# Grid attention with q and k projected by feature: no turns, a new order on VectorE, and parts cut one step apart

## The chip, the cores and the metric

The kernel runs on one core of one Trainium2 chip. The metric is the device time of one execution in microseconds (us), as the median of the runs shown. The core has TensorE (PE in the profile; PEld is its weight load), VectorE (DVE), ScalarE (ACT), GpSimd (POOL) and SyncE (SP); each runs its own queue of instructions in order, and they wait for each other by semaphores. Data lies in SBUF (128 partitions); TensorE writes its results to PSUM, eight banks of 512 float32 values per partition.

## The reference

Two blocks of two layers each, on 512 tokens of width 1024 (the second block has 256 context tokens besides), all in float32. The part that the change touches is the last layer of the second block: 16 heads of 64 attend from a grid of 8 rows x 64 columns to a window of neighbours, with a relative bias, and to all context tokens.

```python
def neighbourhood_latent(q, k, v, kc, vc, rpb):
    ...
        s_loc = jnp.einsum('bqhd,bkhd->bhqk', qr, kr).astype(jnp.float32) * scale + bias.astype(jnp.float32)
        s_loc = jnp.where(mask, s_loc, -jnp.inf)
        s_ctx = jnp.einsum('bqhd,blhd->bhql', qr, kc).astype(jnp.float32) * scale
        p = jax.nn.softmax(jnp.concatenate([s_loc, s_ctx], axis=-1), axis=-1)
        p_loc = p[..., :kh * GRID_W].astype(vr.dtype)
        p_ctx = p[..., kh * GRID_W:].astype(vc.dtype)
        return jnp.einsum('bhqk,bkhd->bqhd', p_loc, vr) + jnp.einsum('bhql,blhd->bqhd', p_ctx, vc)

def c_mixer(u, uc, in_w, out_w, rpb, need_ctx):
    ...
    o = neighbourhood_latent(q, k, v, k_c, v_c, rpb)
    y = (o * jax.nn.silu(z)) @ out_w
```

With 8 grid rows and a window 8 rows high, each query sees all 512 latent keys, masked by column, and 256 context keys: 768 in all.

## The kernel before

The kernel is a list of stages (`layers`, `block_two`), played one after the other on every engine. A stage waits for the one before it, unless it is `joined`.

**Precision.** Float32 products are made of three fast ones. Each operand is split into a high part (rounded to the format `fp32r`, by a ScalarE copy) and a low part (operand minus high part, on VectorE). `three` (line 516) issues high x high, high x low and low x high into the same bank.

**Products** (`Product`). Weights come in pieces of 1 MB through two buffers `w_raw`; ScalarE cuts `w_high` (L476), VectorE `w_low` (L481), and TensorE multiplies while the next piece is cut. In mode "tok" the tokens are stationary, 128 at a time, and the result has tokens on partitions. In mode "feat" the weights are stationary and the result has features on partitions; with 768 tokens (`spill`) each feature tile needs two banks, one of 512 and one of 256 columns. The stages ahead of the grid attention make the gate z (feat), q, k and v (all tok), each in two groups. `CopyOut` copies finished banks out, by turns on ScalarE and VectorE (L1125, L1127, L1129).

**Grid attention** (`WidePairs` with `grid=True`, built by `grid_units`). It has 8 units, a unit being two heads (`m` = 0, 1), and 4 query blocks of 128 in each, so 32 steps. A step's scores for both heads fill three banks (512 latent keys, 256 context keys, 256 context keys, 512 latent keys); steps use banks 0 to 2 and 3 to 5 by turns. Bank 6 collects the output of a unit, bank 7 is for small turns. In iteration s:

- TensorE: `scores(s + 1)` (12 matmuls, L1822, which wait until the banks of step s - 1 have been copied out by both engines), `turn_probs(s)` (12 transposes of 128x128 back into the same banks, L1856; the first four wait for the first head's exp, the others for the second's), one `turn` of q or k of the next unit (L1801), `values(s - 1)` (24 matmuls, L1873), and at the end of a unit `wide` (L1881): four transposes of the inverse sums, which wait for `staged_ready`.
- VectorE: at the end of a unit `gate_wide` (L2095, inverse sums times gate z) and `invert` (L2052 reciprocal, L2057 widening copy, which signals `staged_ready`); `maxima(s + 1)`: the maximum over the context columns (L2023, `sink_part`), then per head one pass that adds the bias in place and takes the maximum (L2034) and a negation (L2036); `copy_probs(s)` (L2064, the first bank of turned probabilities, signals `turned_ready`); `low_turned` (L2073, L2079), the low part of what was turned.
- ScalarE: `copy_probs(s)` (L1945, the other two banks), `copy_turned` (L1921, the high part of what was turned), `exps(s + 1)` (L1934, two, one per head), and at the end of a unit the copy of the output (L1952) and the issue of the loads of z (L1967) and of bias tiles (L1972).
- GpSimd: the final product of a unit (L2131) and the mask on a bias tile (L2141).

q and k lie by token in `q_c` and `k_c`, but the scores need them by feature, with q's columns in each grid row reversed. So for every unit TensorE turns 128 columns of q (4 transposes) and of k (4 and 2) through bank 7 ("turns"; the entries of `turns` name the iteration), ScalarE copies the high part to `q_high` and `k_high`, and VectorE writes the low part in place over the turned columns:

```python
turns.append((4 * p - 4, p, q_high[:, p % 2, 0:4, :], lambda x, p=p: q_c[:, x, P * p:P * p + P], P, 4, None, "back"))
```

The three turns of the first unit stand ahead of the loop, followed by ten matmuls without use (`keep_warm`, L523).

## Time and profile before

| | |
|---|---|
| median of 3 runs (lowest, highest) | 2335.25 us (2334.78, 2335.45) |
| the profiled execution | 2336.09 us |
| its span | 2334.3 us |
| busy: TensorE, VectorE, ScalarE, GpSimd | 2248.6 (96%), 1297.0 (56%), 925.0 (40%), 272.2 (12%) us |
| chain that ended last | PE 80%, DVE 10%, ACT 5% |
| mean granted clock of TensorE | 0.994 |

The span is the stretch from the first to the last instruction of one profiled execution; that execution took 1.8 us more than its span, and 0.84 us more than the median. All times of rows count from the start of the span. Matmuls are pipelined, so a matmul's duration overlaps with that of the next; the distance of two starts tells what one costs. TensorE's 96% is therefore no proof that it is the bound everywhere: the chain of work that ended last is followed back from the last instruction, at each step to whatever released it, and it shows who was waited for. Products fill most of the span; the grid attention runs from about 2112 to 2282 us. A row of a timeline gives start, duration, engine, line, operation, what it writes and reads, its shape and, in brackets, the idle time before it with what ended it. "ACTq" and "issue" are the time of an engine's instruction queue, not of its arithmetic.

### The profile page before, as it was taken

How to read it: one execution, taken by the hardware profiler on the slowest of the kernel's cores; microseconds unless marked ns; L12 is line 12 of the kernel's file. 1: busy time of each engine (PE TensorE's matmuls, PEld its weight loads, DVE VectorE, ACT ScalarE, POOL GpSimd, SP SyncE). 2: the span in 40 equal slices, each digit the busy share in tenths (PEclk: the TensorE clock that was granted, in tenths of full speed). 3: DMA queues.
4: the chain of work that ended last, by engine and by line, in shares of the span. 5: the costliest groups of instructions: out<-in, count | busy, mean ns of one | idle time of the engine just before them, and what ended most of it. 6: DMA issues, size and time to landing. Idle time of an engine off the chain costs nothing.

```text
span 2334.3 us, 32859 instructions
## 1 busy us (share of the span) xinstructions
PE 2248.6 (96%) x13409; PEld 1859.1 (80%) x13409; DVE 1297.0 (56%) x1890; ACT 925.0 (40%) x1564; POOL 272.2 (12%) x175
## 2 busy tenths in 40 slices
PE   6999999999999999999999999999899999999998
PEld 5876688888888776788888888897787878887777
DVE  4687458963225778369943255216666363126774
ACT  3447742222214357542222232324655242115663
POOL 2001222211002012132211000000000000001220
PEclk9999999999999999999999999999999999999999
DMA  5210035532223210145523321320000224213321
GB/s 157 86 68 2 1 104 182 184 109 90 108 94 94 81 37 2 37 144 171 172 90 108 108 65 51 101 87 13 15 15 15 93 82 141 72 55 75 54 57 55
DMA packets 146088, 191.10 MB, mean 82 GB/s; under 512 B 42229, under 2 KB 95490, under 8 KB 145922
## 3 DMA queue, kind: packets, MB, share of 16 engines
q1 hardware_dynamic: 110288, 169.83, 22.0%
q10 hardware_dynamic: 35586, 19.01, 3.5%
q8 instruction: 106, 1.74, 0.3%
q14 instruction: 44, 0.36, 0.0%
q0 software_dynamic: 64, 0.16, 0.0%
HBM read 181.51 MB, written 7.48 MB: 81 GB/s over the span
## 4 chain that ended last, share of the span: by engine, by line
PE 80%; DVE 10%; ACT 5%; issue 3%; DMA 1%; POOL 1%; ACTq 1%; POOLq 0%; DVEq 0%
PE ps L516 63%; PE ps L1822 3%; PE ps L2391 2%; PE ps L2408 2%; DVE ps L2034 2%; PE ps L2420 2%; DVE probs_t L2064 1%; DVE neg_max L2015 1%; ACT probs L1934 1%; PE ps L1856 1%; PE ps L2396 1%; PE ps L723 1%; DVE sink_part L2023 1%; DVE w_low L481 1%; ACT probs_t L2497 1%
## 5 line engine op out<-in xcount | busy, mean ns | idle before, releaser
L481 DVE TENSOR_TENSOR w_low<-w_raw,w_high 128x2048 fp32r<-128x2048 f32 (+4 forms) x140 | 305.7, 2184 | 497.9 <-ACT w_high L476 497.7
L476 ACT ACTIVATE w_high<-w_raw 128x2048 fp32r<-128x2048 f32 (+4 forms) x140 | 252.9, 1807 | 614.0 <-PE ps L516 603.5
L516 PE MATMUL ps<-h_hi,w_high 128*128 128x512 f32 x976 | 371.7, 381 | 1.6 <-DVE h_lo L2788 0.8
L516 PE MATMUL ps<-h_lo,w_high 128*128 128x512 f32 x976 | 369.1, 378 | 0.0
L516 PE MATMUL ps<-h_hi,w_low 128*128 128x512 f32 x976 | 369.0, 378 | 0.0
L516 PE MATMUL ps<-w_high,h_hi 128*128 128x512 f32 (+3 forms) x736 | 277.4, 377 | 7.8 <-DVE w_low L481 7.1
L516 PE MATMUL ps<-w_low,h_hi 128*128 128x512 f32 (+3 forms) x736 | 274.7, 373 | 0.0
L516 PE MATMUL ps<-w_high,h_lo 128*128 128x512 f32 (+3 forms) x736 | 274.6, 373 | 0.0
L516 PEld LDWEIGHTS ps<-h_hi,w_high 128*128 128x128 f32 x976 | 183.7, 188 | 37.6 <-DVE w_low L481 1.9
L516 PEld LDWEIGHTS ps<-h_hi,w_low 128*128 128x128 f32 x976 | 183.6, 188 | 34.8
L516 PEld LDWEIGHTS ps<-h_lo,w_high 128*128 128x128 f32 x976 | 183.7, 188 | 34.1 <-issue 0.5
L516 PEld LDWEIGHTS ps<-w_high,h_hi 128*128 128x128 f32 x736 | 138.9, 189 | 36.5 <-DVE w_low L481 7.8
L516 PEld LDWEIGHTS ps<-w_low,h_hi 128*128 128x128 f32 x736 | 138.8, 189 | 22.6
L516 PEld LDWEIGHTS ps<-w_high,h_lo 128*128 128x128 f32 x736 | 138.9, 189 | 21.6
L710 DVE SCALAR_TENSOR_TENSOR ada_acc<-ada_w,cond,ada_acc 128x512 f32<-128x512 f32 x168 | 143.6, 896 | 2.5
L1462 POOL TENSOR_TENSOR gated<-gated,inv_wide 128x512 f32<-128x512 f32 x44 | 95.3, 2186 | 374.2 <-ACT gated L1454 374.2
L516 PE MATMUL ps<-act_hi,w_low 128*128 128x512 f32 x352 | 137.0, 389 | 0.0
L516 PE MATMUL ps<-act_hi,w_high 128*128 128x512 f32 x352 | 136.9, 389 | 0.0
L516 PE MATMUL ps<-act_lo,w_high 128*128 128x512 f32 x352 | 136.9, 389 | 0.0
L1934 ACT ACTIVATE probs<-ps,neg_max 128x768 f32<-128x768 f32 (+3 forms) x160 | 123.6, 783 | 13.7 <-DVE neg_max L2019 7.9
L1945 ACT ACTIVATE probs_t<-ps 128x1024 f32<-128x1024 f32 (+2 forms) x68 | 56.0, 823 | 131.7 <-PE ps L1856 131.7
L1457 ACT ACTIVATE act_hi<-gated 128x512 fp32r<-128x512 f32 x44 | 27.7, 632 | 198.3 <-DVE gated L1475 197.3
(360 smaller groups left out, 3905.3 us busy)
## 6 DMA issues: line engine op xcount, KB each, us to landing
w_raw<-in_w_gate_up SPq DMA_DIRECT2D x44, 1024.0 KB, 5.1
ada_w<-in_ada_w SPq DMA_DIRECT2D x24, 1024.0 KB, 5.1
w_raw<-in_w_down SPq DMA_DIRECT2D x20, 1024.0 KB, 4.8
w_raw<-in_w_in SPq DMA_DIRECT2D x16, 1024.0 KB, 5.1
w_raw<-in_c_in_w SPq DMA_DIRECT2D x16, 1024.0 KB, 5.6
w_raw<-in_w_out SPq DMA_DIRECT2D x8, 1024.0 KB, 4.8
w_raw<-in_ab_in_w SPq DMA_DIRECT2D x8, 1024.0 KB, 5.1
bias<-bias_scratch ACTq DMA_DIRECT2D x32, 224.0 KB, 4.8
```

What stands on the lines that cost most here:

```text
L476: e.activation(w_high[j % 2][:, 0:size], w_raw[j % 2][:, 0:size], ACT.Copy).then_inc(sig.w_high_done, 1)
L481: e.tensor_tensor(w_low[j % 2][:, 0:size], w_raw[j % 2][:, 0:size], w_high[j % 2][:, 0:size].bitcast(F32), ALU.subtract).then_inc(sig.w_lo ...
L516: mm = e.matmul(dst, lhs, rhs, start=start and a == 0, stop=stop and a == 2)
L710: ins = e.scalar_tensor_tensor(out=acc, in0=w, scalar=c, in1=acc, op0=ALU.mult, op1=ALU.add)
L1462: e.tensor_tensor(gated[:, m, :], gated[:, m, :], inv_wide[:], ALU.mult).then_inc(sig.silu_scaled, 1)
L1822: return e.matmul(dst.rearrange("p (b c) -> p b c", c=P), q(m, block), k(m, a, b), start=n == 0, stop=stop and n == 2)
L1934: ins = e.activation(self.probs[s % 2][:, r * n:(r + 1) * n], self.row(s, r), ACT.Exp, bias=neg_max2[:, c:c + 1], accum_out=sums2[:, c:c + 1])
L1945: e.activation(self.probs_t[s % 2][:, a:b], flat[:, self.base(s) + a:self.base(s) + b], ACT.Copy).then_inc(sig.turned_second, 1)
L2034: ch.step(e.tensor_tensor_reduce(a, a, bias, 1.0, seed2[:, c], ALU.add, ALU.max, max2[:, c]))
L2391: e.matmul(ps[:, self.bank(s, m), 0:n], q[x.rows(m), t * P:n], k[x.rows(m), 0:n], start=True, stop=False)
L2408: mm = e.transpose(ps[:, self.bank(s, m), kt * P:(kt + 1) * P], probs1[s % 3][:, m, kt * P:(kt + 1) * P], ident)
L2420: mm = e.matmul(ps[64 * m:64 * m + 64, 6, t * P:(t + 1) * P], x.value(m, kt), probs_t1[s % 2][:, m, kt * P:(kt + 1) * P], start=kt == 0, s ...
```

## The change

**q and k by feature.** Both products change to mode "feat": q is scaled and reversed by column when it is copied out, and k is made with two banks per feature tile. The turns, their copies and low parts go, and with them the ten `keep_warm` matmuls ahead of the loop.

**Parts.** The high part of a unit's q and k is now one ScalarE copy each from `q_c` and `k_c` (SBUF), the low part one VectorE subtraction each in place (512 and 768 columns). For the first unit this is done in a new stage `PairAhead` between the products of k and v, into buffers of its own. For unit p the high parts of q and k stand behind the exps in iterations 4p - 5 and 4p - 4 (`cut_at`), the low parts at the end of VectorE's iterations 4p - 4 and 4p - 3.

**Order on VectorE.** In iteration s: context maximum of step s + 1, copy of the turned probabilities of step s, the two bias passes of step s + 1, then `invert`, `gate_wide` and the low part.

```diff
-        q_c = at("q_c", [P, NT, DM], F32, B1)
-        k_c = at("k_c", [P, NA, DM], F32, B1 + 16384)
+        q_c = at("q_c", [P, KD, S], F32, B1)
+        k_c = at("k_c", [P, KD, ALL], F32, B1 + 16384)
...
+        q_first = at("q_first", [P, NT, P], F32R, B1 + 65536)
+        k_first = at("k_first", [P, NA, P], F32R, ROWS_AT)
...
+                self.cut_at = {4 * p - 5 + c: (p, c) for p in range(1, U) for c in range(2)} if grid else {}
...
-                keep_warm(e, 6, 10 if self.grid else 4)
+                if not self.grid:
+                    keep_warm(e, 6, 4)
...
+                    if s in self.cut_at:
+                        p, c = self.cut_at[s]
+                        if p >= 2:
+                            e.wait_ge(sig.scores_ready, B["scores_ready"] + 4 * (p - 2) + 4)
+                        pair_high(e, p, c)
...
+                def context_max(s):
+                    two, b = slice(self.col[s], self.col[s + 1]), self.base(s)
+                    e.wait_ge(sig.scores_ready, B["scores_ready"] + s + 1)
                     ch.step(e.tensor_reduce(out=seed2[:, two], in_=flat[:, b + 512:b + 1024].rearrange("p (m n) -> p m n", m=2),
                                             op=ALU.max, axis=AX.X))
+
+                def grid_max(s, m):
+                    (u, js), b = self.steps[s], self.base(s)
                     j = js[0]
-                    if j == 0:
+                    if j == 0 and m == 0:
                         e.wait_ge(sig.bias_masked, B["bias_masked"] + u)
                     ch.wait(e)
...
+                def grid_iteration(s):
+                    if s == self.N:
+                        gate_piece(e, {n: B[n] for n in ("gate_landed", "pair")}, 1, gate_row, 3)
+                    if s + 1 < self.N:
+                        context_max(s + 1)
+                    if 0 <= s < self.N:
+                        copy_probs(s)
+                    if s + 1 < self.N:
+                        grid_max(s + 1, 0)
+                        grid_max(s + 1, 1)
+                    if s in self.ends:
+                        invert(self.ends[s])
+                    if s - 1 in self.ends:
+                        gate_wide(self.ends[s - 1])
+                    if s - 1 in self.cut_at:
+                        p, c = self.cut_at[s - 1]
+                        pair_low(e, B, p, c, 2 * (p - 1) + c + 1)
...
+        def pair_high(e, p, c):
+            src, high, _ = pair_parts(p, c)
+            e.activation(high, src, ACT.Copy).then_inc(sig.qk_high, 1)
+
+        def pair_low(e, B, p, c, n):
+            src, high, low = pair_parts(p, c)
+            e.wait_ge(sig.qk_high, B["qk_high"] + n)
+            e.tensor_tensor(low, src, high.bitcast(F32), ALU.subtract).then_inc(sig.qk_ready, 1)
...
-            from_in("tok", 0, 512, CopyOut(lambda i, m, t0: q_c[:, m, ds(i * 512, 512)], HD ** -0.5), w="c_in_w_2", groups=2, joined=True),
-            from_in("tok", DM, 512, CopyOut(lambda i, m, t0: k_c[:, m, ds(i * 512, 512)]), w="c_in_w_2", groups=2, tokens=ALL, joined=True),
+            from_in("feat", 0, 512, CopyOut(lambda i, m, t0: q_c[:, i * 4 + m, :].rearrange("p (r c) -> p r c", c=64), HD ** -0.5, view=backwards),
+                    w="c_in_w_2", groups=2, joined=True),
+            from_in("feat", DM, 512, CopyOut(lambda i, m, t0: k_c[:, i * 4 + m, t0:(S if t0 == 0 else ALL)]), w="c_in_w_2", groups=2, tokens=ALL, joined=True),
+            PairAhead(),
```

VectorE at the end of the first unit, in the kernel before (`sums_194` and `inv_stage_192` belong to that unit; the reduction, the two `ISA` passes with their read-outs and negations are the maxima of the next unit's first step; `probs_t` is the copy of turned probabilities):

```order
L2052 RECIPROCAL sums_inv_195<-sums_194 128x8 [waits probs_ready]
L2057 COPY inv_stage_192<-sums_inv_195 128x512 [waits vec_steps]
L2023 TENSOR_REDUCE sink_part<-ps 128x2 [waits scores_ready]
L2034 ISA ps,max_197<-ps,bias_1_154,sink_part 128x512 [waits bias_masked,vec_steps]
L2034 ISA max_197 128x1
L2036 TENSOR_SCALAR neg_max_193<-max_197 128x1 [waits vec_steps]
L2034 ISA ps,max_197<-ps,bias_1_154,sink_part 128x512
L2034 ISA max_197 128x1
L2036 TENSOR_SCALAR neg_max_193<-max_197 128x1 [waits vec_steps]
L2064 COPY probs_t_1_169<-ps 128x512 [waits o_ready,probs_turned]
```

and now:

```order
L2032 TENSOR_REDUCE sink_part<-ps 128x2 [waits scores_ready]
L2075 COPY probs_t_1_169<-ps 128x512 [waits o_ready,probs_turned]
L2045 ISA ps,max_199<-ps,bias_1_154,sink_part 128x512 [waits bias_masked,vec_steps]
L2045 ISA max_199 128x1
L2047 TENSOR_SCALAR neg_max_195<-max_199 128x1 [waits vec_steps]
L2045 ISA ps,max_199<-ps,bias_1_154,sink_part 128x512 [waits vec_steps]
L2045 ISA max_199 128x1
L2047 TENSOR_SCALAR neg_max_195<-max_199 128x1 [waits vec_steps]
L2063 RECIPROCAL sums_inv_197<-sums_196 128x8 [waits probs_ready]
L2068 COPY inv_stage_194<-sums_inv_197 128x512 [waits vec_steps]
```

The copy of turned probabilities moved from behind the two bias passes to ahead of them, and the reciprocal and its widening copy from ahead of the maxima to behind them.

TensorE at the start of the grid stage, before (`con` is the identity matrix, `band_r,ident_r` the matmuls without use, the last row the first scores):

```order
L1801 MATMUL ps<-con,q_c 128x128 [waits evac_vec,bank_done,evac_act]
L1801 MATMUL ps<-con,q_c 128x128 x3
L1801 MATMUL ps<-con,k_c 128x128 x6
L523 MATMUL ps<-band_r,ident_r 128x384 x10
L1822 MATMUL ps<-k_high,q_high 128x512 [waits qk_ready]
```

and now:

```order
L1826 MATMUL ps<-k_first,q_first 128x512 [waits evac_vec,bank_done,evac_act,qk_ready]
L1826 MATMUL ps<-k_first,q_first 128x256
L1826 MATMUL ps<-kc_low,q_first 128x256
L1826 MATMUL ps<-kc_low,q_first 128x512
L1826 MATMUL ps<-k_first,qc_low 128x256
```

The ten transposes and the ten matmuls without use are gone, and the stage's first matmul is one of the scores.

## Rows read from the trace of the kernel before

**Rows 1.** The chain that ended last, grid attention: start us, us, what
```profile
2133.21 1.42 PE ps L1822 x9
...
2158.64 1.43 PE ps L1822 x9
2160.09 0.70 DVE sink_part L2023
...
2163.67 1.43 PE ps L1822 x9
...
2270.77 1.41 PE ps L1822 x9
```
**Rows 2.** Timeline, end of the third unit, TensorE's weight loads and VectorE
```profile
2174.05 0.19 PEld L1822 LDWEIGHTS ps<-k_high,q_high 64*128 64x128 f32 x2 [1.05 <-DVE kc_low L2079]
...
2174.70 0.20 DVE L2052 RECIPROCAL sums_inv<-sums 128x8 f32<-128x8 f32 x1 [0.70 <-ACT probs L1934]
...
2175.01 0.43 DVE L2057 COPY inv_stage<-sums_inv 128x512 f32<-128x512 f32 x1
...
2175.39 1.30 PEld L1856 LDWEIGHTS ps<-con,probs 128*128 128x128 f32 x12
...
2176.37 0.76 DVE L2034 CUSTOM_DVE_ANT_0 ps<-ps,bias,sink_part 128x512 f32<-128x512 f32 x1 [0.17 <-DVE sink_part L2023]
2176.86 1.29 PEld L1873 LDWEIGHTS ps<-probs_t,v_c 128*64 128x64 f32 x24 [0.17 <-issue]
...
2177.38 0.76 DVE L2034 CUSTOM_DVE_ANT_0 ps<-ps,bias,sink_part 128x512 f32<-128x512 f32 x1
...
2178.32 0.42 PEld L1881 LDWEIGHTS ps<-con,inv_stage 128*128 128x128 f32 x4 [0.17 <-issue]
2178.32 0.69 DVE L2064 COPY probs_t<-ps 128x512 f32<-128x512 f32 x1
```
**Rows 3.** Timeline, first steps of the stage
```profile
2112.05 0.42 PEld L1801 LDWEIGHTS ps<-con,q_c 128*128 128x128 f32 x4 [1.41 <-issue]
...
2113.47 0.33 ACTq L1967 DMA_DIRECT2D z_unit<-z_scratch  x1
...
2113.82 3.35 ACTq L1972 DMA_DIRECT2D bias<-bias_scratch  x4
...
2117.38 0.76 DVE L2034 CUSTOM_DVE_ANT_0 ps<-ps,bias,sink_part 128x512 f32<-128x512 f32 x1 [0.17 <-DVE sink_part L2023]
...
2118.49 0.90 ACT L1934 ACTIVATE probs<-ps,neg_max 128x768 f32<-128x768 f32 x1
...
2123.88 0.91 ACT L1934 ACTIVATE probs<-ps,neg_max 128x768 f32<-128x768 f32 x1
...
2124.93 0.86 PEld L1856 LDWEIGHTS ps<-con,probs 128*128 128x128 f32 x8 [0.32 <-ACT probs L1934]
...
2126.06 1.02 ACT L1945 ACTIVATE probs_t<-ps 128x1024 f32<-128x1024 f32 x1 [1.18 <-PE ps L1856]
```
**Rows 4.** Stretches: us, busy by engine (instructions), granted clock, DMA share, GB/s
```profile
1880.00:1890.00 10.00, 8.78 (x46) 7.74 (x44) 4.82 (x13) 1.99 (x5) 0.00 (x0) 0.83 0.00 0
2128.00:2271.00 143.00, 132.31 (x1437) 111.92 (x1438) 110.28 (x265) 90.11 (x169) 32.84 (x13) 1.00 0.32 60
```
**Rows 5.** The chain again: a 768-token feature product, then the products before the grid
```profile
1486.57 67.15 PE ps L516 x384
...
1949.91 161.17 PE ps L516 x711
```
**Rows 6.** Timeline at 701 us: VectorE with and without GpSimd beside it
```profile
700.90 0.74 DVE L1587 SCALAR_TENSOR_TENSOR h_lo<-x_t,cols,h_hi 128x512 fp32r<-128x512 f32 x1
...
703.87 1.18 DVE L1587 SCALAR_TENSOR_TENSOR h_lo<-x_t,cols,h_hi 128x512 fp32r<-128x512 f32 x1
...
701.33 8.30 POOL L1598 TENSOR_TENSOR square_sum<-square_sum,gated 128x512 f32<-128x512 f32 x5 [122.29 <-ACT gated L1572]
```
**Rows 7.** Timeline behind the grid: low parts from SBUF, back to back
```profile
2284.50 4.91 DVE L1657 TENSOR_TENSOR oc_lo<-o_all,oc_hi 128x512 fp32r<-128x512 f32 x8 [3.87 <-ACT oc_hi L1650]
```

More of the change, by code:

```diff
@@ L180, in build_program @@
         con = fixed("con", [P, CONST_W])
+        ROWS_AT = off[0]
         rows = fixed("rows", [P, DEPTH, ROW_W])
@@ L1914, in copy_turned @@
                     src = ps[0:rows_, bank, 0:n * P]
-                    if kind == "back":
-                        src, dst = backwards(src), dst.rearrange("p b (r c) -> p (b r) c", c=64)
-                    elif kind == "two":
+                    if kind == "two":
                         src = src.rearrange("p (m b c) -> p m b c", m=2, c=P)
@@ L2006, in maxima @@
                     e.wait_ge(sig.scores_ready, B["scores_ready"] + s + 1)
-                    if not self.grid:
-                        scored, top, own = flat[:, self.start(s):self.start(s) + self.total(s)], neg_max2[:, two], sink[:, x.head:x.head + 2]
-                        if tiles == 1:
-                            scored, by_head = scored.rearrange("p (m n) -> p m n", m=2), top
-                        else:
-                            scored = scored.rearrange("p (m t n) -> p m t n", m=2, t=tiles)
-                            by_head, top = top.rearrange("p (t m) -> p m t", m=2), top.rearrange("p (t m) -> p t m", m=2)
-                            own = bc(own.unsqueeze(1), [P, tiles, 2])
-                        ins = e.tensor_reduce(out=by_head, in_=scored, op=ALU.max, axis=AX.X, negate=True)
-                        if x.kind == "window":
-                            ch.step(ins)
-                            ch.wait(e)
-                            ins = e.scalar_tensor_tensor(out=top, in0=own, scalar=-1.0, in1=top, op0=ALU.mult, op1=ALU.min)
-                        ins.then_inc(sig.max_ready, 1)
-                        return
@@ L2022, in maxima @@
-                    b = self.base(s)
+                    scored, top, own = flat[:, self.start(s):self.start(s) + self.total(s)], neg_max2[:, two], sink[:, x.head:x.head + 2]
+                    if tiles == 1:
+                        scored, by_head = scored.rearrange("p (m n) -> p m n", m=2), top
+                    else:
+                        scored = scored.rearrange("p (m t n) -> p m t n", m=2, t=tiles)
+                        by_head, top = top.rearrange("p (t m) -> p m t", m=2), top.rearrange("p (t m) -> p t m", m=2)
+                        own = bc(own.unsqueeze(1), [P, tiles, 2])
@@ new lines, in maxima @@
+                    ins = e.tensor_reduce(out=by_head, in_=scored, op=ALU.max, axis=AX.X, negate=True)
+                    if x.kind == "window":
+                        ch.step(ins)
+                        ch.wait(e)
+                        ins = e.scalar_tensor_tensor(out=top, in0=own, scalar=-1.0, in1=top, op0=ALU.mult, op1=ALU.min)
+                    ins.then_inc(sig.max_ready, 1)
+                def context_max(s):
+                    two, b = slice(self.col[s], self.col[s + 1]), self.base(s)
+                    e.wait_ge(sig.scores_ready, B["scores_ready"] + s + 1)
@@ L2069, in low_turned @@
                     e.wait_ge(sig.qk_high, B["qk_high"] + i + 1)
-                    if kind == "back":
-                        tiles = lambda a: a.rearrange("p b (r c) -> p b r c", c=64)
-                        src = src.rearrange("p (b r c) -> p b r c", r=2, c=64)[:, :, :, ::-1]
-                        e.tensor_tensor(tiles(lows), src, tiles(high.bitcast(F32)), ALU.subtract).then_inc(sig.qk_ready, 1)
-                    elif kind == "two":
+                    if kind == "two":
                         src = src.rearrange("p (m b c) -> p m b c", m=2, c=P)
@@ L2103, in vector @@
                     low_turned(i, i)
+                def grid_iteration(s):
[15 more added lines that the diff above has]
+                        pair_low(e, B, p, c, 2 * (p - 1) + c + 1)
+                if self.grid:
+                    for s in range(-1, self.N + 1):
+                        grid_iteration(s)
+                    return
                 for s in range(-1, self.N + 1):
-                    if self.grid and s == self.N:
-                        gate_piece(e, {n: B[n] for n in ("gate_landed", "pair")}, 1, gate_row, 3)
                     if s - 1 in self.ends:
@@ L2118, in vector @@
                         low_turned(i, 7)
-                    if not self.grid and self.N - 6 <= s < self.N - 2:
+                    if self.N - 6 <= s < self.N - 2:
                         low_part(s - self.N + 6)
```

63 lines of the change are left out of this document (38 added, 25 removed).

## The prediction

> **What bounds the kernel now.** I read the page first for where TensorE is not saturated, then the chain that ended last through the grid attention, then the timeline of one step there. The products are bound by TensorE alone (one chain piece of 711 matmuls lasts 161.17 us, 0.2267 us each [rows 5]). The grid attention is different. It has 32 steps (8 head pairs of 4 query blocks). Call S(n) the start of step n's scores on TensorE. S(4) is at 2133.21, S(31) at 2270.77 [rows 1]: 137.56 us for 27 steps. Within a plain step (S at 2158.64, next at 2163.67, 5.03 us [rows 1]) the chain goes from the scores to the context maxima C after 1.45, then through the two bias passes G0 and G1 (a pass takes 1.01 to the next one, 0.94 to what follows the second [rows 2]), then the copy D of the turned probabilities (0.69), then the next scores, which overwrite the banks that D empties. So VectorE's order C, G0, G1, D is the bound: D, which releases TensorE, stands behind both bias passes. Every fourth step is some 0.3 us longer by the lower part of k.
>
> **What limits when D moves ahead.** The new order is C, D, G0, G1. The loop scores, C, D becomes 1.45 + 0.61 + 0.75 = 2.8 us (0.61 is the spacing of back-to-back 512-wide VectorE instructions, eight in 4.91 [rows 7]). Three other limits take over. VectorE's own work: 0.61 + 0.70 + 1.01 + 0.94 = 3.26. ScalarE and TensorE in turn: exp of the second head starts, 1.05 later TensorE turns the second part, 1.13 after that the 1.02 us copy A starts [rows 3], then both exps again, the second 0.88 behind the first: 1.05 + 1.13 + 0.93 + 0.88 = 3.99 (0.93 and 0.88: A's 1.02 and an exp's 0.91, each overlapping its successor by some hundredths). TensorE's own queue: scores to transposes T 1.34, T to values V 1.47, V to whatever follows 1.46 [rows 2]: 4.27. TensorE is the longest, so a plain step should take **4.27**.
>
> **The end of a pair breaks this.** After the fourth block TensorE's queue holds W, four transposes of the inverse sums, in front of the next scores. W waits for VectorE's reciprocal and its widening copy. Before, these stand ahead of the maxima and are done at 2175.44, long before TensorE comes to W at 2178.32 [rows 2]. Now they stand behind G1. Worked from S = 0: C 1.45, D 2.06 (it also needs the first four of the twelve transposes, T + 0.73, an estimate from a third of T's 1.30 and 0.3 from issue to result: 2.07), G0 2.76, G1 3.77, reciprocal 4.71, widening copy done 0.74 later at 5.45 (0.31 + 0.43 [rows 2]), W starts 0.06 later. W holds the queue 0.42, and 0.17 for the next wait, so the next scores start at **6.10** and not at 4.27: a new wait of 1.83 per pair.
>
> The three steps behind it, by the same offsets: S 6.10, T 7.44, C 7.55, D 8.17 (by the transposes), G0 8.87, G1 9.88. Behind G1 VectorE has the gate product (0.61) and the lower part of q (0.61), so the next C waits until 12.04 rather than 11.82. S 10.37 (TensorE's queue), D 12.65, G0 13.35, exp 14.46 (1.11 behind G0, from 2117.38 to 2118.49 [rows 3]). ScalarE copies k's high part (0.82, an estimate from 0.60 for 512 columns) and then the unit's output behind its exps, ending at 13.24. The first V of the next pair waits for that output copy to free its bank, until 13.30 instead of 13.18. So S 14.76, then 19.03. **One pair takes 6.10 + 4.27 + 4.39 + 4.27 = 19.03 us**; plain limits are met elsewhere (the lower part of k, 0.92 by 1.5 x 0.61, fits in front of a C that is due 1.45 behind its scores). From S(4) to S(31) are six such pairs and the first three steps of a seventh: 6 x 19.03 + 14.76 = 128.9 against 137.56. **Gain 8.6.**
>
> **Start of the stage.** Before, TensorE begins with ten transposes at 2112.05, and ScalarE's queue starts the loads of gate and bias at 2113.47, behind three copies; its first exp is 5.02 later, at 2118.49 [rows 3]. Now the turns are gone and the first pair's parts are made under the value product, so scores start at about 2112.1. The exp is then bound by the same 5.0 us of issue and table load from 2112.1: 2117.1, 1.4 earlier. From there: second turns at +1.93, A at +3.06 (2120.2), S(2) 1.08 behind A's start (1.02 and 0.06 to TensorE) at 2121.24, S(3) at 2125.5 and S(4) at 2129.8 by the queue. S(4) was 2133.21: **gain 3.4**.  The ten keep-warm matmuls taken out lay before work that waited anyway and give nothing by themselves.
>
> **The turns, highs and lows inside the steps.** Per pair ten transposes leave TensorE; in the sum they are simply absent from the 4.27. ScalarE's high parts (1.42 a pair instead of 1.57) sit between its exps and A, where it waits 1.13 for the turns anyway. The four bias issues (3.35 for four at the start [rows 3]) begin while the first exp runs and end about when A is due; they fall into the step that W stretches. Edits with no price: the maxima of the other attention are the same code, and the first pair's buffer in the rows of norm weights is dead by then.
>
> **The products.** q by feature has the same 192 matmuls of 512 columns. k by feature has 192 of 512 and 192 of 256 columns instead of 288 of 512. The trace has that very shape: 384 matmuls in 67.15 us [rows 5]. Old: 288 x 0.2267 = 65.3. **Loss 1.9.** The copies of k and the two new parts per engine (about 1.5 us) push the next weight cut by some 2 us; that half is wanted 16 us (72 x 0.2267) later and takes 1.92 + 2.29, so it is hidden; without that cover it would cost 2.
>
> **A price that the trace of the grid stage doesn't show.** The lower parts now read two operands from SBUF, and GpSimd masks bias tiles in the same steps. Elsewhere a 128x512 VectorE instruction with two SBUF inputs takes 0.74 with GpSimd idle and 1.18 beside a GpSimd sum [rows 6]. By that k's lower part grows from 0.92 to about 1.58 once per pair. It delays C to within the step where W makes TensorE wait 1.8 us, so I take 0; uncovered it is 7 x 0.66 = 4.6, and I keep that as the upper bound. The Trainium skill, GPSIMD Engine Reference, section 1 (Specifications), says the SBUF interfaces are shared with VectorE, with contention when a VectorE instruction has two SBUF inputs. Here that speaks against moving the source of the lower parts from PSUM to SBUF; the rows on the two durations agree with it, and by it alone the sum would lose at most those 4.6.
>
> **Tail.** G0 and G1 of the last step start 0.1 later relative to the scores and the second exp then trails G1: loss 0.3. The last reciprocal has to follow D, but TensorE reaches W only after V.
>
> **Sum.** 8.6 + 3.4 - 1.9 - 0.3 = 9.8 us. The profiled execution took 2336.09 (span 2334.3), so 2326.3; the median of the runs, 2335.25, is 0.84 below it, so **2325.4**. Own bounds: the wait at W ±0.3 a pair (2), the plain step 4.2 to 4.45 (up to 4 the wrong way, for 21 steps), the contention up to 4.6, the start ±1.5. Together 2320.5 to 2331.
>
> **Rivals.**
> - *The wait at W costs nothing.* If the steps behind it win back the 1.83 because something other than TensorE's queue bounds a step, the gain grows by 7 x 1.83 = 12.8: 2312.6. For it: ScalarE's loop is 3.99, 0.28 a step shorter, so VectorE and ScalarE do catch up. Against it: the queue itself has no slack to give back. Half of it would give 2319. Chance 0.12 for both.
> - *The chain is not broken.* TensorE's scores wait for A as well as for D. If A comes late in each step (exp behind G1, turns behind scores), the old mean of 5.09 (137.56 / 27) falls to about 5.0 only, and of the start the first 1.6 is won: 27 x 0.09 + 1.6 - 1.9 - 0.3 = 1.8, or 2333.4. Against it: A's loop is 3.99 when nothing else interferes. Chance 0.12.
> - *Slower: the granted clock falls at the new wait.* Between 1880 and 1890 us, where TensorE has waits between keep-warm matmuls and one-column sums, the granted clock averages 0.83 [rows 4], part of the time at 1.2 GHz instead of 2.4: 10 x 0.17 = 1.7 us of work lost. If W's wait (1.25 us of idle) did that once in each of seven pairs and at the start, it costs 8 x 1.7 = 13.6: 2339. It turns the gain into a loss from six falls on. Against it: TensorE now has up to 0.76 us free in every step (5.03 less 4.27) and the clock of the grid stage is 1.00 [rows 4], and the new steps hold less waiting in sum. Chance 0.05. The Trainium skill, TensorE: Matmul & The Clock Gate, Part 4: PE-mode transpose, says transposes don't count as work for the clock as matmuls do; in the old stage T alone takes 1.30 of each 5.03 us at a granted 1.00, so that rule has little weight here; by it the start and the pairs' ends would be as in this rival.
>
> **How the numbers follow.** Forecast 0.66, no cost at W 0.12, steps near 5 0.12, clock 0.05; 0.05 stays for a wait that I don't see, on either side. The range of 8 in 10 takes in more than half of the first rival's gain and nearly reaches the second rival: **2317.5 to 2332.5**. About 0.2%, 4.7 us, is what a measurement here can tell from no change: faster below 2330.6, slower above 2339.9. Steps near 5 fall within 0.2%, and so does the upper end of the forecast's own range. Faster 0.82, same 0.14, slower 0.04.
>
> **What the profile after would show.** Scores start every 4.27 us in plain steps, and the engine's idle time before them is near 0; before W TensorE idles 1.2 to 1.3 us with the reciprocal's copy as releaser, seven times; from S(4) to S(31) 129 us; first scores some 1.0 behind the value product's end; the k product 67.2 us. If W's wait is absent or the step is under 4.2, TensorE's queue was costed wrong; if scores are released by VectorE's copies, the order did not help as said; if k's lower part lasts over 1.5 and C follows it, the contention reached the path.

## The result and the profile after

The changed kernel took 2339.14 us (median of 8 runs, 2337.66 to 2342.48) where the kernel before took 2334.71 beside it: ratio 1.0021, 95% interval 1.0013 to 1.0030. The forecast was 2325.4 and faster, with a range of 2317.5 to 2332.5. The profiled execution took 2337.66, its span is 2335.9 at a granted clock of 0.994. Of one version below (invert ahead), two of eleven executions took 5746 and 6967 us; its ratio leaves them out, and its median without them is 2334.70.

Where the time went, after beside before, all in microseconds of the two traces. The k product takes 66.9 for 65.3 (+1.6), the value product 65.5 for 65.4. From the start of the last copy of v to S(4), the scores of step 4, it is 20.5 for 22.1 (-1.6). From S(4) at 2130.86 to S(31) at 2272.34 it is 141.48 for the 137.56 of [rows 1] (+3.9), and the forecast was 128.9. From there to the end it is 63.6 for 63.5. (The k product began 2.4 earlier in this execution of after, mostly by shorter landings of the gate z ahead of q, which the change doesn't touch.)

First the chain of after at the end of its last pair but one and in the last pair. Columns: start us, us, what; the chain starts a piece where the one before it ends, so matmuls can stand 0.07 later than in a timeline.
```profile
2262.67 0.44 DVE inv_stage L2068
2263.11 0.14 issue
2263.24 0.63 PE ps L1885 x4
2263.88 1.34 PE ps L1826 x9
2265.22 1.46 PE ps L1860 x12
2266.68 1.46 PE ps L1877 x24
2268.14 1.35 PE ps L1826 x9
2269.49 1.46 PE ps L1860 x12
2270.95 1.46 PE ps L1877 x24
2272.41 1.34 PE ps L1826 x9
```
In this stretch the order of the queue is as forecast: scores, transposes and values follow one another on TensorE, 4.26 and 4.27 a step for the 5.03 of [rows 1], and W (L1885) starts behind the copy of the inverse sums. The last pair is the one in which no parts for a further pair are made. In the steps from 4 to 27, where they are made, the chain reads otherwise, once in four steps:
```profile
2144.75 0.76 DVE ps L2045
2145.51 0.07 DVE max L2045
2145.60 0.15 DVE neg_max L2047
2145.76 1.00 DVE kc_low L2181
2146.76 3.04 issue
2149.80 0.68 DVE sink_part L2032
```
and the timeline of after at the same place has, of VectorE and GpSimd (start us, us, engine, line, operation):
```profile
2145.04 4.02 POOL L2204 TENSOR_TENSOR bias<-bias,con 128x1792 f32<-128x1792 f32 x1
...
2145.67 4.20 DVE L2181 TENSOR_TENSOR kc_low<-k_c,k_high 128x768 fp32r<-128x768 f32 x1
...
2149.80 0.68 DVE L2032 TENSOR_REDUCE sink_part<-ps 128x2 f32<-128x512 f32 x1
```
The lower part of k took 4.20 us. GpSimd's bias mask had begun 0.63 before it and ended at 2149.06, and the lower part ended 0.81 after that. All the lower parts of one line in after, then in the kernel with the mask in eight pieces (the view of one tile; ns minimum/median/maximum, first and last start):
```profile
L2181 DVE TENSOR_TENSOR kc_low<-k_c,k_high x7: 948/4173/4399, 2127.2 to 2251.7; 128x768 fp32r<-128x768 f32 x7
L2181 DVE TENSOR_TENSOR kc_low<-k_c,k_first x1: 957/957/957, 2047.0 to 2047.0; 128x768 fp32r<-128x768 f32 x1
```
```profile
L2181 DVE TENSOR_TENSOR kc_low<-k_c,k_high x7: 948/949/1104, 2126.0 to 2239.1; 128x768 fp32r<-128x768 f32 x7
```
In after it is 0.95 where no mask runs and over 4 in the six pairs; the forecast had put 1.58 as its worst. The first lower part of q in the loop meets a mask too, and takes 3.57 for 0.68. In the kernel before, the lower part of q of the same size, read out of PSUM, begins 1.20 into the same mask and is not slowed (timelines of before, then of after):
```profile
2121.95 4.02 POOL L2141 TENSOR_TENSOR bias<-bias,con 128x1792 f32<-128x1792 f32 x1 [170.30 <-DMA bias<-bias_scratch]
...
2123.15 0.69 DVE L2073 TENSOR_TENSOR qc_low<-ps,q_high 128x512 fp32r<-128x512 f32 x1 [0.35 <-ACT q_high L1921]
```
```profile
2119.58 4.03 POOL L2204 TENSOR_TENSOR bias<-bias,con 128x1792 f32<-128x1792 f32 x1 [170.49 <-DMA bias<-bias_scratch]
...
2120.60 3.57 DVE L2181 TENSOR_TENSOR qc_low<-q_c,q_high 128x512 fp32r<-128x512 f32 x1
```

### The profile page after: what moved, and what is told of

Same layout as the page of the kernel before. It is cut to its first block, busy times and chain, and to the rows that moved or that the text cites. A ratio compares the mean times of both kernels' runs of the same rounds, so it can differ in the third digit from the quotient of the medians.

```text
span 2335.9 us, 32840 instructions
## 1 busy us (share of the span) xinstructions
PE 2240.4 (96%) x13415; PEld 1854.0 (79%) x13415; DVE 1312.4 (56%) x1884; ACT 928.1 (40%) x1558; POOL 272.4 (12%) x175
## 4 chain that ended last, share of the span: by engine, by line
PE 80%; DVE 9%; ACT 5%; issue 4%; POOL 1%; ACTq 1%; DMA 1%; POOLq 0%; DVEq 0%
PE ps L519 64%; PE ps L2454 2%; PE ps L1826 2%; PE ps L2471 2%; PE ps L2483 2%; PE ps L1860 1%; DVE ps L2045 1%; DVE neg_max L2022 1%; ACT probs L1937 1%; PE ps L2459 1%; PE ps L726 1%; PE ps L1877 1%; ACT probs_t L2560 1%; DVE w_low L484 1%; DVE probs_t L2075 1%
## 5 line engine op out<-in xcount | busy, mean ns | idle before, releaser
L519 PE MATMUL ps<-h_hi,w_high 128*128 128x512 f32 (+1 forms) x1168 | 439.7, 376 | 2.4 <-DVE w_low L484 1.4
L519 PE MATMUL ps<-h_lo,w_high 128*128 128x512 f32 (+1 forms) x1168 | 437.2, 374 | 0.0
L519 PE MATMUL ps<-h_hi,w_low 128*128 128x512 f32 (+1 forms) x1168 | 436.8, 374 | 0.0
L519 PEld LDWEIGHTS ps<-h_hi,w_high 128*128 128x128 f32 x1168 | 220.0, 188 | 44.0 <-DVE w_low L484 2.8
L519 PEld LDWEIGHTS ps<-h_hi,w_low 128*128 128x128 f32 x1168 | 219.8, 188 | 39.8
L519 PEld LDWEIGHTS ps<-h_lo,w_high 128*128 128x128 f32 x1168 | 220.0, 188 | 39.0 <-issue 0.5
L519 PE MATMUL ps<-w_high,h_hi 128*128 128x512 f32 (+3 forms) x576 | 214.8, 373 | 5.9 <-DVE w_low L484 5.2
L519 PE MATMUL ps<-w_low,h_hi 128*128 128x512 f32 (+3 forms) x576 | 212.3, 369 | 0.0
L519 PE MATMUL ps<-w_high,h_lo 128*128 128x512 f32 (+3 forms) x576 | 212.0, 368 | 0.0
L1860 PE MATMUL ps<-con,probs 128*128 128x128 f32 x784 | 103.9, 280 | 8.9 <-ACT probs L1937 8.9
```

The lines of the kernel that those rows point to most:

```text
L519: mm = e.matmul(dst, lhs, rhs, start=start and a == 0, stop=stop and a == 2)
L1860: mm = e.transpose(flat[:, self.base(s) + b * P:self.base(s) + (b + 1) * P], self.probs[s % 2][:, b * P:(b + 1) * P], ident)
```

## The experiments

**The question.** Theory H: a VectorE instruction with two inputs in SBUF is held until the GpSimd instruction beside it ends. Rivals: S, it is slowed at a rate while GpSimd works; W, its own size makes it slow; and for the pairs, that the wait of TensorE's W or the place in the order costs. "C to C" below is the start of the context reduction (`sink_part`, 128x512) of step 4 to that of step 31 in the profiled execution; before and after have 137.56 and 141.48. "Pair" is the usual distance over four steps. Ratios are to the kernel before on the same chip.

| kernel | median us | ratio, 95% | pair | C to C |
|---|---|---|---|---|
| after | 2339.14 | 1.0021 (1.0013 to 1.0030) | 21.05 | 141.48 |
| mask in 8 pieces | 2323.99 | 0.9951 (0.9938 to 0.9965) | 18.82 | 127.51 |
| mask in 2 pieces | 2324.50 | 0.9952 (0.9940 to 0.9965) | 19.15 | 129.77 |
| mask of 1 row in 14 | 2323.40 | 0.9948 (0.9936 to 0.9961) | 18.81 | 127.49 |
| lower parts off the mask | 2325.23 | 0.9959 (0.9946 to 0.9971) | 18.91 | 128.12 |
| invert ahead | 2334.81 | 0.9998 (0.9989 to 1.0007) | 20.44 | 137.42 |
| lower parts off the mask, invert ahead | 2316.37 | 0.9919 (0.9906 to 0.9933) | 17.73 | 120.64 |
| mask in 8, invert ahead | 2316.09 | 0.9916 (0.9903 to 0.9930) | 17.65 | 119.49 |
| the same, two issues moved | 2313.30 | 0.9905 (0.9891 to 0.9918) | 17.65 | 119.52 |
| before, order alone | 2356.19 | 1.0090 (1.0076 to 1.0104) | 24.6, 23.2 | 158.25 |
| before, order, products first | 2327.97 | 0.9965 (0.9952 to 0.9979) | 19.30 | 129.46 |
| after, old order | 2345.66 | 1.0048 (1.0035 to 1.0060) | 21.6, 23.0 | 149.10 |

**Mask in eight pieces.**
```diff
-            e.tensor_tensor(b, b, cm, ALU.add).then_inc(sig.bias_masked, 1)
+            for m0, m1 in ((0, 1), (1, 2)):
+                for r0, r1 in ((0, 4), (4, 8), (8, 11), (11, 14)):
+                    cm = colmask.unsqueeze(1).unsqueeze(1).to_broadcast([P, m1 - m0, r1 - r0, 64])
+                    e.tensor_tensor(b[:, m0:m1, r0:r1, :], b[:, m0:m1, r0:r1, :], cm, ALU.add).then_inc(sig.bias_masked, 1)
```


> The changed kernel, its bias mask (one GpSimd instruction of 4.02 us a pair) cut into eight GpSimd instructions of some 0.5 us over the same rows. Theory H (a VectorE instruction with two inputs in SBUF is held until the GpSimd instruction that runs beside it has ended): the lower part of k that took 4.20 us is held for one piece, takes 0.95 to 1.6 us, a pair takes 19.0 to 19.5 us for 21.05, and the kernel some 7 x 1.8 us less, 2323 to 2329. Rival S (the two engines share a path, so that the lower part is slowed as long as GpSimd is at work): it stays at 3.5 to 4.2 us, a pair at 21, the time at 2337 to 2341. Rival W (the lower part is slow by its own size of 128x768): the same as S.

The lower part of k takes 0.95, a pair 18.82, the time is in the range that H gave. S is out: GpSimd is at work all the while beside the lower part, and the lower part is not slowed. W is out: the size is the same. The timeline of this kernel:
```profile
2144.13 5.22 POOL L2207 TENSOR_TENSOR bias<-bias,con 128x256 f32<-128x256 f32 x7
...
2144.76 0.95 DVE L2181 TENSOR_TENSOR kc_low<-k_c,k_high 128x768 fp32r<-128x768 f32 x1
```
The first piece ends at 2144.86, and the lower part at 2145.71. Now it is GpSimd that waits: the piece that begins beside the lower part takes 1.48 and ends 0.60 behind it. Of the 56 pieces the shortest takes 0.585 and the longest 1.507 (median 0.722).

**Mask in two pieces**, one head each.
```diff
+            for m0, m1 in ((0, 1), (1, 2)):
+                for r0, r1 in ((0, 14),):
```

> The changed kernel with the mask in two GpSimd instructions (one head each, some 2.0 us) instead of one of 4.02 or eight of 0.5. Theory H (held until the GpSimd instruction beside it has ended, whose own length is the price): the lower part of k starts some 0.6 us into the first and takes 1.4 + 0.8 = 2.2 us, half of the 4.2; a pair 19.0 to 19.7; the kernel 2325 to 2330. Rival S (slowed at a rate as long as GpSimd is at work, 4.0 us in all): 3.5 to 4.2 us, a pair 20.5 to 21, 2334 to 2339.

The dose fits H:
```profile
2144.51 4.89 POOL L2207 TENSOR_TENSOR bias<-bias,con 128x896 f32<-128x896 f32 x2
...
2145.14 2.30 DVE L2181 TENSOR_TENSOR kc_low<-k_c,k_high 128x768 fp32r<-128x768 f32 x1
2147.36 0.68 DVE L2032 TENSOR_REDUCE sink_part<-ps 128x2 f32<-128x512 f32 x1
```
The shortest piece takes 2.11, so the first ends at 2146.62, and the lower part ends at 2147.44, again 0.82 later; 2.2 was expected. The two pieces take 4.89 for the 4.02 of one, for the most part because the second waits for the lower part: it takes 2.82 for 2.12. The hold of 1.35 costs only 0.33 a pair (19.15 less 18.82), the hold of 3.25 costs 2.23: most of a short one is absorbed by the slack of VectorE, which a long one uses up. The median is half a microsecond under the range that H gave.

**Mask of one row in fourteen** (13 of the 14 rows of each head's bias stay without the column mask; 0.45 us on GpSimd).
```diff
-            e.tensor_tensor(b, b, cm, ALU.add).then_inc(sig.bias_masked, 1)
+            e.tensor_tensor(b[:, :, 0:1, :], b[:, :, 0:1, :], cm, ALU.add).then_inc(sig.bias_masked, 1)
```

> The changed kernel with only the first of the 14 rows of each head's bias masked, so that the GpSimd instruction takes some 0.3 to 0.4 us; 13 of 14 rows of the column mask are left out. Theories H and S both: the lower part of k takes 0.95 to 1.2 us, a pair 19.03 us as the sum in the prediction had it, the kernel 2323 to 2327. Rival W (slow by its own size): 4.2 us and 2337 to 2341. If the lower part is short and a pair still takes over 20 us, the sum in the prediction has a second fault.

A pair of 18.81 as with eight pieces, 2323.40. The forecast's sum for the pair (19.03) has no second fault of size: from scores to scores its steps read 6.02, 4.26, 4.27, 4.26 here for the 6.10, 4.27, 4.39, 4.27 of the prediction. The first four steps take 18.67 here for 17.74 with eight pieces, because the granted clock averages 0.77 in the second of them and 1.00 there; two kernels with other masks show the same fall (last section).

**Lower parts off the mask.**
```diff
-                self.cut_at = {4 * p - 5 + c: (p, c) for p in range(1, U) for c in range(2)} if grid else {}
+                self.cut_at = {max(4 * p - 6, -1) + c: (p, c) for p in range(1, U) for c in range(2)} if grid else {}
+                self.low_at = {max(4 * p - 5, 1) + c: (p, c) for p in range(1, U) for c in range(2)} if grid else {}
...
-                    if s - 1 in self.cut_at:
-                        p, c = self.cut_at[s - 1]
+                    if s in self.low_at:
+                        p, c = self.low_at[s]
```


> The changed kernel with the high parts of q and k of a pair one step earlier on ScalarE and so the lower parts one step earlier on VectorE, ahead of the mask (the second pair's lower parts, which cannot come earlier, one step later, behind it). Mask and lower parts keep their sizes. H and S: the lower parts take 0.68 and 0.95 us (up to 1.5 where the 1.28 us product of GpSimd is beside one), a pair 19.0 to 19.6, the kernel 2323 to 2329. Rival W: 4.2 us wherever it stands, 2337 to 2341. Rival P (the place in the order costs, not the length: the lower part ahead of invert or of the last product delays TensorE's W): lower parts short, a pair over 20.

Mask (4.03) and lower parts (0.95, 0.68) keep their sizes and only no longer meet: 2325.23. With the pieces this shows by two independent edits that the meeting is the price, and the times that H gave hold in both (the pairs came out 0.1 to 0.2 shorter than its 19.0). The second pair's lower part of k is late for its scores once (TensorE waits 1.25 for it).

**Invert ahead of the maxima.**
```diff
                         copy_probs(s)
+                    if s in self.ends:
+                        invert(self.ends[s])
                     if s + 1 < self.N:
                         grid_max(s + 1, 0)
                         grid_max(s + 1, 1)
-                    if s in self.ends:
-                        invert(self.ends[s])
```


> The changed kernel with invert (sums inverted, copied wide) ahead of both heads' maxima, behind the copy of the turned probabilities. TensorE's W need no longer wait for it, which was 1.83 us of the 6.1 us step; the maxima come some 0.6 us later. If the wait at W is on the path by itself: the W step falls from 6.0 to 4.3 to 4.9, a pair by 1.1 to 1.8, the kernel by 8 to 13, to 2326 to 2331. Rival: the exponentials then come later and the next step takes back what W gives: a pair within 0.5 of 21.05, the kernel 2335 to 2340. The held lower part stays at 4.2 us in either.

It came out between the two and in neither range for a pair: TensorE no longer waits at W, yet the W step goes only from 6.32 to 5.7, and a pair to 20.44. Where the step is not behind a held lower part, in the first pair, it is 4.86. Behind one, maxima and exponentials are still late, and they hold the next scores in W's place. With the hold gone, the same edit gives its full 1.2 a pair:

> Lower parts one step earlier, off the mask, and invert ahead of both heads' maxima. The run with the lower parts moved alone gave a pair of 18.9 us, of which 6.03 is the step with TensorE's W; with invert ahead in the uncut mask that step was 5.7 because VectorE was late from the hold, and 4.86 (4.27 of the plain step and 0.59 for W) in the first pair, where no hold stood before it. If that reading holds: W step 4.9 to 5.2, a pair 17.7 to 18.1, the kernel 7 x 1.0 less than 2325, 2317 to 2320. Rival: the step after W takes back what W gives (VectorE is 0.6 later): a pair 18.7 or more, 2323 to 2326.

> Mask in eight pieces and invert ahead of both heads' maxima. Cut alone gave a pair of 18.82 us with a W step of 6.02. If W's wait is on the path by itself: W step 4.86 to 5.0, a pair 17.7, the kernel 7 x 1.1 below 2324, 2315 to 2318. Rival: taken back in the next step, a pair 18.5 or more, 2321 to 2324.

They read W steps of 4.86 and 4.85 and pairs of 17.73 and 17.65, and both are faster than the kernel before by 0.8%. The first is 0.6 under the range given for its time, though its profiled execution held a fall of the granted clock in the second step (0.77), which the other has not. What TensorE waits for at W, in after and then in mask in 8 with invert ahead (the view of line 1885: us, times):
```profile
L1885 PE MATMUL ps<-con,inv_stage x28: 272/273/329, 2136.2 to 2263.6; 128*128 128x128 f32 x28
its engine sat idle before it (us, times) until:
  DVE inv_stage L2068: 5.2, 7
  issue: 4.2, 6
```
```profile
L1885 PE MATMUL ps<-con,inv_stage x32: 272/273/330, 2136.5 to 2260.4; 128*128 128x128 f32 x32
its engine sat idle before it (us, times) until:
  issue: 1.4, 8
```

**Two bias issues moved.** In the kernel before and in after, ScalarE issues four bias loads and loads its table ahead of the first exponentials. After, timeline at the start:
```profile
2111.66 3.34 ACTq L1975 DMA_DIRECT2D bias<-bias_scratch  x4
...
2114.62 0.76 DVE L2045 CUSTOM_DVE_ANT_0 ps<-ps,bias,sink_part 128x512 f32<-128x512 f32 x1
...
2115.03 1.28 ACT L1937 ACT_TABLE_LOAD   x1 [6.78 <-issue]
...
2116.32 0.90 ACT L1937 ACTIVATE probs<-ps,neg_max 128x768 f32<-128x768 f32 x1
```
```diff
                 load_z(0)
                 if self.grid:
-                    load_bias(1)
+                    load_bias(1, (0,))
...
                     if s + 1 < self.N:
                         exps(s + 1)
+                    if s == -1 and self.grid:
+                        load_bias(1, (1,))
```


> Mask in eight pieces, invert ahead of the maxima, and two of the four bias transfers that ScalarE issues at the start of the stage moved behind its first exponentials. With all four ahead of them ScalarE issued from 2114.64 to 2118.22 and loaded its table until 2119.53, while the first maximum was there at 2117.96; two fewer issues end 1.9 us earlier, so the first exponentials start at 2118.0 for 2119.54. If that is on the path: 1.5 us less than mask in pieces with invert ahead, 2313 to 2316 beside 2316.1. Rival: the mask of the second pair then comes 3.3 us later and is late for the second pair's first maximum, or the copy of the probabilities waits for the moved issues: the same or up to 1 us more, 2316 to 2318.

The first exponentials start 1.90 behind the first context reduction for 3.45 with all four, and the first four steps take 16.20 for 17.63. The stretch behind is unchanged (119.52 and 119.49). So 1.4 us was won by the edit; the rest of the 2.8 between the two medians lies elsewhere, and the two ran on different chips. This is the fastest version tried, 0.95% under the kernel before.

**The order alone, on the kernel before** (turns and lower parts out of PSUM stay).
```diff
+                    if self.grid:
+                        if s + 1 < self.N:
+                            context_max(s + 1)
+                        if 0 <= s < self.N:
+                            copy_probs(s)
+                        if s + 1 < self.N:
+                            grid_max(s + 1)
...
                     if s in self.ends:
                         invert(self.ends[s])
+                    if s - 1 in self.ends and self.grid:
+                        gate_wide(self.ends[s - 1])
```


> The kernel before with the order of VectorE alone changed (the copy of the turned probabilities ahead of both heads' maxima; invert and the gate's product behind them); the turns of q and k on TensorE and the lower parts out of PSUM stay. Theory: the chain of 5.03 us is broken, but TensorE's queue then holds the turns, 0.60, 0.60 and 0.38 us: 6.02 + 4.87 + 4.87 + 4.65 = 20.4 us a pair, as before: 2332 to 2337. The lower parts out of PSUM are not held by the mask. Rival: the turns hide in waits of TensorE, a pair of 18.8 to 19.4, 2324 to 2328.

Both expectations missed. A pair is 24.6 or 23.2, with one step of 8.85. TensorE's turn of q needs bank 7, which the gate's product sets free, and that product now stands behind both maxima (the view of line 1801 in this kernel):
```profile
its engine sat idle before it (us, times) until:
  DVE wide L2100: 31.4, 12
who waited for it (us, times):
  ACT q_high L1921: 14.2, 6
```
(The 31.4 counts matmuls and weight loads both, so some 15, or 2.50 in each of six pairs.) The pairs of 23.2, with a step of 7.42, ran at a granted clock of 1.00. In the pairs of 24.6 the clock fell behind the same idle time (0.81 over the step of 8.85), and the turn and the values behind it take 1.4 longer. So the bank is the cause up to 23.2, and the clock of the rest. The cure for that place was then run:
```diff
                     if self.grid:
+                        if s - 1 in self.ends:
+                            gate_wide(self.ends[s - 1])
+                        if s in self.ends:
+                            invert(self.ends[s])
                         if s + 1 < self.N:
                             context_max(s + 1)
```

> The kernel before with the copy of the turned probabilities ahead of both heads' maxima, as in the run of the order alone, but the gate's product and invert left ahead of the reduction of the context, where the kernel before has them. The order alone gave pairs of 24.6 and 23.2 us, because TensorE's turn of q waits for the bank that the gate's product, then behind both maxima, sets free (step of 8.85 us, 2.5 us of wait at L1801). If that is the whole cause: steps of 4.7 to 5.1, no step over 6, a pair of 19.4 to 20.4, the kernel 2328 to 2336. Rival (the turns' own chain TensorE, ScalarE, VectorE costs on in other steps): a pair over 20.6, 2337 to 2350.

Steps of 4.70, 4.69, 4.70 and 5.21, a pair of 19.30, the kernel 0.35% faster than before: a little better than the forecast on both counts. The lower parts out of PSUM that meet the same mask of 4.02 take 0.68 and 0.69 us (128x512); they have one input in SBUF and are not held.

**By feature alone, with the old order.**
```diff
+                    if s - 1 in self.ends:
+                        gate_wide(self.ends[s - 1])
+                    if s in self.ends:
+                        invert(self.ends[s])
                     if s + 1 < self.N:
                         context_max(s + 1)
-                    if 0 <= s < self.N:
-                        copy_probs(s)
-                    if s + 1 < self.N:
                         grid_max(s + 1, 0)
                         grid_max(s + 1, 1)
+                    if 0 <= s < self.N:
+                        copy_probs(s)
```

> The changed kernel with the old order of VectorE (gate's product, invert, both heads' maxima, then the copy of the turned probabilities, the lower parts last). Theory: the chain of 5.02 us a step stands and leaves VectorE no slack, so that the 3.2 us for which the lower part of k is held falls on the path: a pair of 22.5 to 24, the kernel 2346 to 2358. Rival (the hold hides in VectorE's idle time of the old order, 0.8 to 0.9 us a step): a pair of 20.4 to 21.4, 2334 to 2341.

The direction was right, the size a little under the range: pairs of 21.6 and 23.0. The lower part of k starts 1.6 into the mask here and takes 3.20, ending 0.82 behind the mask's end once more. Of the hold, 1.55 a pair reaches the path (the step with it is 6.57 for 5.02). The pairs of 23.0 have a second cause, in the last section.

## Why the prediction was wrong

**The step that failed** is the price of the lower parts' SBUF reads. The prediction had read in [rows 6] that a VectorE instruction goes from 0.74 to 1.18 beside GpSimd, and took that as a rate: k's part 0.92 to 1.58, cost 0, at most 7 x 0.66 = 4.6. The GpSimd instructions of those rows are short (8.30 for 5), and the same trace shows there already what a rate hides, the end of one against the end of the other:
```profile
702.95 1.56 POOL L1598 TENSOR_TENSOR square_sum<-square_sum,gated 128x512 f32<-128x512 f32 x1
...
703.87 1.18 DVE L1587 SCALAR_TENSOR_TENSOR h_lo<-x_t,cols,h_hi 128x512 fp32r<-128x512 f32 x1
```
GpSimd ends at 704.51 and VectorE 0.55 later, and so does each of the five; q's held lower part, of the same 128x512, also ends 0.55 behind its mask. The mask is one instruction of 4.02, and the runs show that the price is the rest of the instruction that stands beside: 3.25 a pair. The assumption that it ends in the step where W waits failed too. It delays the context reduction, the copy and then the maxima; the following steps read 7.23, 3.12 and 6.32 for 4.16, 4.26 and 6.02, so 3.07 is lost, 1.14 won back and 0.30 lost again: 2.23 a pair. From step 4 to step 31 that is 13.4 of the 13.97 between after and mask in eight pieces (141.48, 127.51); a fall of the granted clock in one step of after (6.88 for 6.32) holds the other 0.56. In the first four steps the two kernels differ by a further 1.8, where the lower part of q is held. The sum, 15.8, stands against 15.2 between the two medians. With the meeting taken out by any of three edits the medians are 2323.40 to 2325.23, beside the forecast of 2325.4: the rest of the sum was sized right (below).

**The chain of 5.03 broken: right.** 4.26 to 4.27 in a plain step of after, on TensorE's queue.

**The new wait at W: right.** The step was forecast at 6.10 and is 5.88 (2130.86 to 2136.74) in the first pair of after, 6.02 in the later pairs where nothing is held. The releaser is the copy of the inverse sums, which [rows 2] had done long before W. The idle time at W is 8.9 over eight waits, 1.1 each, with the mask in pieces (1.2 to 1.3 was said); in after it is less, 5.2 over seven, because the hold has made TensorE late as well. The rival that it costs nothing is refuted: to remove it gave 1.2 a pair.

**The stage from step 4 on, without the hold:** forecast 128.9, measured 127.5. The step that was to wait for the output copy, 4.39, reads 4.26 or 4.27.

**Start of the stage:** forecast a gain of 3.4, 1.6 came; S(4) stands 20.5 behind the last copy of v for 18.7. The first exponentials are where they were put, 5.96 behind that copy (2116.32 less 2110.36) for 6.0. The missing 1.8 is the held lower part of q: with the mask in eight pieces the first four steps take 17.7, in after 19.6, and S(4) stands 18.67 behind the last copy of v (2111.29 to 2129.96). That the bias issues bound this place was seen in the prediction and not followed further; moving two of them gave another 1.4.

**The products:** forecast a loss of 1.9 for k, measured 1.6, as 384 matmuls of the two widths. **Tail:** no difference of the size forecast can be seen (63.6 and 63.5 from step 31).

**The rival of the clock** named 2339, the very time that was measured, and this is chance: it was priced as a fall at each W, and with the mask in pieces, where W waits eight times, the granted clock is 1.00 from step 4 to step 31. After has one fall there, worth 0.56, behind the hold (last section). **The rival of the unbroken chain** (2333.4) would have been nearer than the forecast, for a wrong reason: pairs of after are not steps of 5 but 7.2, 3.1, 6.3 and 4.4.

## What to carry to other kernels

Before moving an operand of a VectorE instruction from PSUM to SBUF, look at which GpSimd instructions run in the same step, and count the length of the longest of them, not a slowdown factor; a trace tells the two apart by the ends (a constant distance from the end of the one to the end of the other is a hold); if they must meet, cut GpSimd's work into instructions of about the length of VectorE's slack. An order that puts a copy ahead moves everything else behind: list for each step moved which bank or buffer it sets free (here bank 7 for the turn of q, the inverse sums for W), since the queue that waits for it pays the whole distance. Where a chain looks right and the time is wrong, look at "issue" behind an instruction that is longer in one place than in another.

## What the runs showed of the hardware

A VectorE instruction with two inputs in SBUF and a GpSimd one on SBUF, as these kernels have them, exclude each other by the whole instruction. VectorE's lower part of k ended 0.81 to 0.82 us behind the end of the GpSimd instruction in three kernels with three different holds (4.20, 3.20 and 2.30 us in all for 0.95 of work), and those of 128x512 ended 0.55 behind it, with GpSimd instructions of 1.56 and 4.03. GpSimd's pieces grow in turn when VectorE is first (the second of two 2.82 for 2.12, one of eight 1.48 for 0.73). VectorE instructions with an input in PSUM ran beside the same mask at their usual length; in the kernel before, whose mask stands from 2166.69 to 2170.72 (timeline):
```profile
2167.02 0.76 DVE L2034 CUSTOM_DVE_ANT_0 ps<-ps,bias,sink_part 128x512 f32<-128x512 f32 x1
...
2168.56 0.68 DVE L2079 TENSOR_TENSOR kc_low<-ps,k_high 128x512 fp32r<-128x512 f32 x1
```
The Trainium skill, GPSIMD Engine Reference, section 1 (Specifications), states the contention for VectorE instructions with two SBUF inputs; the runs agree, and give it a size.

An idle time of TensorE can cost clock. In the old order with the parts by feature, TensorE idles 2.26 us up to 2177.38 and then works slowly; the stretches of that kernel (us, busy by engine, granted clock, DMA share, GB/s):
```profile
2173.00:2177.00 4.00, 2.11 (x30) 1.70 (x28) 3.74 (x9) 2.29 (x4) 0.03 (x1) 1.00 0.00 0
2177.00:2179.00 2.00, 1.62 (x14) 1.41 (x15) 1.11 (x4) 0.68 (x2) 0.00 (x0) 0.97 0.36 82
2179.00:2181.00 2.00, 2.00 (x12) 1.96 (x10) 1.78 (x5) 0.00 (x0) 0.00 (x0) 0.50 1.31 206
2181.00:2183.00 2.00, 2.00 (x24) 1.71 (x24) 1.27 (x4) 1.60 (x2) 0.00 (x0) 0.67 1.30 166
```
The granted clock is 0.50, that is 1.2 GHz, from 2179 on, twelve transposes take 2.67 for 1.53, and the step is 6.47 for 5.01; this makes the pairs of 23.0. After has it once (0.75 over a step of 6.88 for 6.32, behind an idle time of 1.56), invert ahead once (6.66 for 5.7, behind 1.59), and the order alone in three of six pairs, behind 2.50. (Another step of after, 7.45 for 7.22, ran at a granted 1.00: there the lower part began 0.24 earlier in the mask and was held for that much longer.) In the second step of the stage, where TensorE waits some 1.5 us for the first exponentials, the granted clock fell to a mean of 0.77 in the profiled executions of three kernels (mask of one row, lower parts off the mask with invert ahead, after in the old order) and stayed at 1.00 in after and mask in eight, which wait as long. The same idle time brought a fall in some pairs and none in others, and why stays open.
